# Hybrid decoder step on one core: the wait for the first two gathered row blocks stands one expert later in the loading queue

## The reference, cut to what matters

```
u = rmsnorm(h)                       # 576 x 1024
# router: best group of 4, then the best 2 of its 4 experts; combine weights per token
for e in range(16):
    gu  = u @ w_gate_up[e]           # 1024 x 512
    hid = silu(gu[:, :256]) * gu[:, 256:]
    moe = moe + combine[:, e] * (hid @ w_down[e])   # 256 x 1024
h = h + moe
```

## Time and profile before

| | us |
|---|---|
| median of 3 runs | 874.9 (874.32 to 877.71) |
| span of the profiled execution | 872.5 |
| PE busy in it | 854.9 |
| one expert in the steady part | 11.4 |

### The profile page before, as it was taken

One profiled execution on the slowest core, in us unless ns is written; L12 is line 12 of the kernel. 1 busy time (PEld: TensorE's weight loads), 2 busy tenths in 40 slices (PEclk: granted clock), 3 DMA queues, 4 the chain that ended last, 5 costly groups with the idle time before them and its releaser, 6 DMA issues.

```text
span 872.5 us, 11853 instructions
## 1 busy us (share of the span) xinstructions
PE 854.9 (98%) x4645; PEld 556.1 (64%) x4645; DVE 388.7 (45%) x857; ACT 223.3 (26%) x478; POOL 155.1 (18%) x186
## 2 busy tenths in 40 slices
PE   8999999999999999999999999999999999999996
PEld 4546777888799877777777764565444444444452
DVE  3223566677546324566734577364211111104553
ACT  2202152265224210121011101230311111125454
POOL 0324420022243314201300250002000000003000
PEclk9999999999999999999999999999999999999998
DMA  9521343502020201334132221157999999685211
GB/s 362 188 85 65 134 124 134 151 1 105 1 99 3 98 1 44 163 111 150 55 139 96 97 97 76 49 193 276 393 373 371 367 365 371 251 319 169 71 38 48
DMA packets 19814, 135.98 MB, mean 156 GB/s; under 512 B 2512, under 2 KB 3024, under 8 KB 12592
## 3 DMA queue, kind: packets, MB, share of 16 engines
q1 hardware_dynamic: 12176, 103.28, 30.9%
q0 software_dynamic: 5424, 26.45, 8.7%
q10 hardware_dynamic: 2160, 5.51, 2.1%
HBM read 117.83 MB, written 21.60 MB: 160 GB/s over the span
## 4 chain that ended last, share of the span: by engine, by line
PE 43%; DVE 3%; issue 2%; ACT 1%; DMA 1%; POOLq 0%; POOL 0%; DVEq 0%; ACTq 0%
PE single L1250 13%; PE pair L1234 6%; PE pair L1151 6%; PE single L914 6%; PE pair L1352 3%; PE pair L935 2%; PE single L1222 2%; PE pair L1290 2%; PE single L935 2%; PE single L1199 1%; DMA mem<-y_slots,posu 1%; PE single L1160 1%; DVE mem L2322 0%; PE single L1263 0%; DVE mem L2082 0%
## 5 line engine op out<-in xcount | busy, mean ns | idle before, releaser
L734 PE MATMUL pair<-mem 128*128 128x288 f32 x640 | 158.9, 408 | 0.0
L734 PEld LDWEIGHTS pair<-mem 128*128 128x128 f32 x640 | 120.3, 190 | 35.6 <-ACT mem L1373 2.1
L1250 PE MATMUL single<-mem 128*128 128x512 f32 x256 | 112.8, 593 | 0.8 <-DVE mem L2284 0.8
L914 PE MATMUL single<-mem 128*128 128x288 f32 x448 | 110.0, 407 | 0.3
L914 PEld LDWEIGHTS single<-mem 128*128 128x128 f32 x448 | 84.7, 190 | 25.7 <-issue 1.6
L1250 PEld LDWEIGHTS single<-mem 128*128 128x128 f32 x256 | 47.3, 190 | 54.1 <-issue 53.1
L1373 ACT ACTIVATE mem<-single 128x256 f32<-128x256 f32 (+5 forms) x113 | 46.5, 421 | 133.2 <-PE single L1160 48.7
L1373 ACT ACTIVATE mem<-pair 128x512 f32<-128x512 f32 (+5 forms) x85 | 37.8, 495 | 164.0 <-PE pair L734 63.1
L2277 DVE SCALAR_TENSOR_TENSOR mem<-single,mem 128x256 f32<-128x256 f32 x16 | 7.7, 483 | 138.8 <-PE single L1250 126.3
L1352 PE MATMUL pair<-mem 128*128 128x512 f32 (+1 forms) x192 | 63.4, 524 | 1.1 <-DVE mem L2332 1.1
L1234 PE MATMUL pair<-mem 128*128 128x512 f32 x128 | 57.7, 593 | 0.5 <-ACT mem L1373 0.5
(11 more groups left out here) (394 smaller groups left out, 1152.3 us busy)
## 6 DMA issues: line engine op xcount, KB each, us to landing
mem<-in_w_gu SPq DMA_DIRECT2D x16, 2048.0 KB, 9.1
mem<-in_w_down SPq DMA_DIRECT2D x16, 1024.0 KB, 11.8
y_slots<-mem SPq DMA_DIRECT2D x16, 512.0 KB, 3.7
y_slots<-in_zeros POOLq DMA_DIRECT2D x8, 512.0 KB, 8.4
mem<-in_w_ga SPq DMA_DIRECT2D x2, 2048.0 KB, 8.6
mem<-in_w_gb SPq DMA_DIRECT2D x2, 2048.0 KB, 8.4
mem<-in_w_wo SPq DMA_DIRECT2D x2, 2048.0 KB, 8.1
mem<-in_w_pg SPq DMA_DIRECT2D x2, 2048.0 KB, 11.5
```

Of the source, the lines that this page charges most:

```text
L734: last = nc.tensor.matmul(pb[:, hf, 0:HALF], w(k), rhs[:, k, hf * HALF:(hf + 1) * HALF], start=(k == 0), stop=(k == kk - 1))
L914: last = nc.tensor.matmul(single[plan.buf[s]][:, 0:HALF], lhs[:, k, :], rhs[:, k, :], start=(k == 0 and j in (0, 1, 3, 4)), stop=(k == 3), ...
L1250: last = nc.tensor.matmul(single[3][:, :], xT[u % 2][:, k, :], w_gu[u][:, k, :], start=(k == 0), stop=(k == KD - 1))
```

## The change

The wait of SP for the gathers `xg0` and `xg1` moves from ahead of the weights of expert 2 to ahead of those of expert 3.

```
             for e in range(4):
                 mm_wait(sp, free[e])
...
-                if e == 2:
+                if e == 3:
                     sp.wait_ge(sem("xg0"), 16)
                     sp.wait_ge(sem("xg1"), 16)
                 sp.dma_start(w_gu_flat[e], a["w_gu"][e * P:(e + 1) * P, :]).then_inc(sem(f"wgu{e}"), 16)
```

## The result

| | us |
|---|---|
| before, median of 8 runs | 874.9 |
| after, median of 8 runs | 879.2 (876.1 to 882.3) |
| ratio, with 95% interval | 1.0049 (1.0038 to 1.0060) |
| span of the profiled execution, before and after | 872.5, 876.1 |

The change makes the kernel some 4.3 us slower, 3.3 to 5.3 by the interval. The range (874.7 to 879.6) holds the median, but the band of the case that was thought likeliest (876.4 to 878.4) does not, and the time of rival 3, in which PE's clock falls, was 879.2.

What follows compares the result with a forecast made beforehand. PE was taken to bound the kernel, with gather 0 lacking slack. Gain 0; gather 0 landing at 597.5 instead of 595.0 costs 2.5 us, so 874.9 + 2.5 = 877.4 us, range 874.7 to 879.6.

Steps and rivals of the forecast that it cites:

- the case that was thought likeliest: Gather 0 lands 2.5 us late and PE idles that long at expert 0's start: 876.4 to 878.4 us, chance 0.57.
- rival 3: PE's clock falls to half in the gap before expert 0, costing 1.8 us beyond 2.5: 879.2 us, chance 0.13.
- What bounds the kernel: PE, busy 854.9 of 872.5 us; a change counts only where it opens or closes a gap of PE.
- gather 0 has no slack: At expert 0's start, each us by which gather 0 lands later than 595.03 costs the kernel one us.
- No gain: Expert 2's weights, issued at about 579.5 instead of 597.5, were already early enough: gain 0, at most 0.1 us.
- The store: Last `u_rows` store shares engines with expert 2's weights, lands at 591.8 instead of 589.3; gather 0 issued 1.8 us late.
- The gather: Gather 0, issued at about 592.5, shares engines busy to 595.0 and lands at 597.5 instead of 595.0.
- Rival 1: Each DMA engine finishes its part of one transfer before turning to the other queue, nothing moves: 874.9 to 875.4, chance 0.15.
- Rival 2: Gather 0 lands 10.8 us after issue, as gather 3 did, 6.5 us lost: 881.4 us, chance 0.12.

Runs made afterwards that it cites:

- experiment 7: Kernel before with the last row of warm matmuls cut from six to four (first kernel) or five (second): 876.7 us, ratio 1.0024, and 875.6 us, ratio 1.0013.
- experiment 1: The changed kernel measured again without further edits, five rounds: 878.25 us, ratio 1.0048 to before.
- experiment 2: Kernel before with the last row of warm matmuls cut from six to three, transfers unchanged: 876.5 us, ratio 1.0028.
- experiment 6: Two kernels profiled again: first only expert 2's gate/up weights ahead of the wait (store 12.0 us, gather 4.6), then the whole change; no new median given.
- experiment 4: Changed kernel with SP also waiting for the `u_rows` stores ahead of expert 2's weights; gather wait stays ahead of expert 3: 882.5 us, ratio 1.0092.

## Why the prediction was right, and where it was off

- *What bounds the kernel, and that gather 0 has no slack:* right. The gather's lateness appears whole as idle time of PE (2.35 us), and 3.36 us of shift are carried unchanged to 784.
- *No gain:* right. Expert 2's weights go out 18 us sooner, and no wait of PE became shorter.
- *The store:* mechanism right, size near. Landing forecast at 591.8, measured 591.1 in the profile after, 592.4 where it took 12.0 us. Its packets did go one for one with 16 KB packets. Gather 0 was forecast out at 592.5 and went out at 591.4.
- *The gather:* forecast landed at 597.5, measured 597.35. The two parts err in opposite directions (the issue 1.1 us early, the transfer 0.9 us long) and cancel. That the end came out to 0.15 us is partly luck: in the other profiles of the changed kernel with its six warm matmuls the gap was 2.5 and 2.9 us. The forecast reckoned the end from the bytes ahead of the gather; with 1 MB fewer, gate/up weights alone, it came no sooner (gaps of 2.3 us twice), and there nearly the whole loss passes through the store.
- *The term that was missing:* the likeliest case held the clock at full. The median of 879.2 is in the range only because the range took in most of rival 3; it is outside the band of the likeliest case and just where rival 3 put it. It was weighed as the third rival, with 0.13, on the ground that 2.4 us is short of the 2.8 us after which the clock fell at the end of the kernel, and that gaps of about 1 us had left it alone. That was the weak step: one fall and a few survivals were read as a border. The runs show a chance that grows with the gap: it fell in three of the five profiles with a gap of 2.3 to 2.9 us that the change or its gate/up half made, and in the one of 2.0 us, and the list in experiment 7 gives the same picture over all executions. The price was sized well, 1.75 us from the first matmuls of the kernel against 1.6 in the profiles of experiments 1 and 7; but it was 2.9 in experiment 2 and in the first profile of experiment 6. The sum that fits is 2.4 (the gather, by the kernels with the gap filled) + 1.9 (the clock). The 1.9 is the rest up to 4.3 and not a measurement of its own; a gap alone gave 2.4 for it.
- *Rival 1, that the turns hold:* falls. The store takes 1.8 to 3.2 us more, as soon as gate/up weights stand behind those of expert 1. The rule of the Trainium skill ("DMA: Bandwidth & Descriptors", Queues, rings and completion order), that an engine drains some 9 to 17 descriptors of a ring before it turns, would, with one descriptor for each row, have had each engine finish its 8 rows of the store (128 over 16 engines) ahead of expert 2's packets. The store's landing after 10.6 to 12.0 us instead of 8.8 and the packet counts of 79 to 73 don't bear that out here, and the measurement decides. No run shows the order of the packets on a single engine.
- *Rival 2, that the gather starves:* not in the changed kernel, but shown to exist once the weights start just ahead of the gather.

## What to carry to other kernels

A wait in a loading queue may protect not what it waits for but what shares the engines with the transfers behind it: here it kept 3 MB of weights, needed 20 us later, off a store of 0.5 MB and the gather behind it, on which PE depends. Before such a wait is moved, add up the bytes that will then lie ahead of the latency-bound transfer, and follow its chain back to the transfers that it depends on itself. And when a gap is opened in PE, count a part for the clock as well: here that part was some 1.9 us beside a lateness of 2.4, and matmuls that nobody reads, in the gap, gave most of it back.

## What the hardware showed that I had not expected

- The granted clock fell after gaps of 2.0, 2.3, 2.5, 2.6 and 2.9 us, and in two other executions stayed at 1.00 through 2.3 us. It can fall when PE is already at work again: 1.7 us after the restart in experiment 1, 1.6 us after it in the first kernel of experiment 7.
- The time at half clock was about 3.4 us (experiments 1 and 7, and the second profile of 6), 6.8 us (experiment 2 and the first profile of 6) and, with the gap of 5.0 us of experiment 4, about 10 us.
- A transfer of 0.5 MB that took 8.8 us to land took 12.0 us beside 16 KB packets and 9.5 us with the 1 MB of 8 KB packets queued behind. With the whole 3 MB behind it, it took 10.6 to 12.0, no longer than with the 2 MB: in these profiles the size of the rows that share its time counts more than the bytes in the queue.
